# Two transformer blocks on one core: the residual stream kept with its features on the partitions

## What is computed

```python
def _rmsnorm(x, g):
    xf = x.astype(jnp.float32)
    y = xf * lax.rsqrt(jnp.mean(xf * xf, axis=-1, keepdims=True) + RMS_EPS)
    return (y * g.astype(jnp.float32)).astype(x.dtype)

def first_block(...):
    h = x
    h = h + _hybrid_mixer(_rmsnorm(h, norm_mix[l]), w_in[l], ...)
    h = h + _memory_attention(h, mem, norm_mem_q[l], norm_mem_kv[l], w_mem_q[l], w_mem_kv[l], w_mem_o[l])
    h = h + _swiglu(_rmsnorm(h, norm_ffn[l]), w_ffn_in[l], w_ffn_out[l])
    return _rmsnorm(h, norm_final)

def second_block(x, c, w_ada, b_ada, ...):
    mod = einsum(silu(c), w_ada) + b_ada      # 6 x 1024: shifts, scales, gates
    h = _rms(x) * (1.0 + scale_m) + shift_m
    proj = h @ w_in                           # FoX q, k, v, gate, forget; retention q, k, v, gate
    mixed = concat(fox(...), retention(...))
    x = x + gate_m * (mixed @ w_out)
    h = _rms(x) * (1.0 + scale_f) + shift_f
    x = x + gate_f * (square(relu(h @ w_mlp_in)) @ w_mlp_out)
```

## Time and profile before

| | before |
|---|---|
| median of three runs | 883.77 us |
| the three runs | 882.23, 883.77, 889.6 us |
| span of the profiled execution | 881.1 us |
| PE busy | 841.1 us (95%) |
| DVE busy | 591.5 us (67%) |
| ACT busy | 368.0 us (42%) |
| POOL busy | 47.6 us (5%) |
| HBM read | 154.07 MB, 176 GB/s over the span |

### The profile page before, as it was taken

How to read it: one execution, slowest core, us unless ns; L and a number is a source line. 1 busy time by engine, 2 the same in 40 slices (tenths; PEclk the granted TensorE clock), 3 DMA queues, 4 the chain that set the end, 5 groups by cost and what they waited for, 6 DMA issues and landing times.

```text
span 881.1 us, 14098 instructions
## 1 busy us (share of the span) xinstructions
PE 841.1 (95%) x5941; PEld 783.2 (89%) x5941; DVE 591.5 (67%) x873; ACT 368.0 (42%) x469; POOL 47.6 (5%) x59
## 2 busy tenths in 40 slices
PE   6999999999998899999999999999897999999997
PEld 6999898999897889999999799989885999999996
DVE  4967667666685558879786686546666778755553
ACT  5467133653464523333333364445542533343331
POOL 0000000002400000000000200200022000000001
PEclk9999689999998999999999999999899899999999
DMA  8944342242443077676776344342323357645421
GB/s 327 365 170 141 138 144 96 88 152 97 196 187 144 1 278 294 237 295 242 272 298 239 144 144 150 139 145 82 111 96 143 139 197 279 248 152 185 186 96 48
DMA packets 23582, 156.03 MB, mean 177 GB/s; under 512 B 3560, under 2 KB 3808, under 8 KB 5344
## 3 DMA queue, kind: packets, MB, share of 16 engines
q1 hardware_dynamic: 23520, 155.13, 47.9%
HBM read 154.07 MB, written 1.05 MB: 176 GB/s over the span
## 4 chain that ended last, share of the span: by engine, by line
PE 78%; DVE 10%; ACT 5%; issue 3%; POOL 2%; DMA 1%; SPq 0%; DVEq 0%; ACTq 0%; POOLq 0%
PE bank L611 15%; PE bank L612 15%; PE bank L613 15%; PE bank L654 7%; PE bank L655 7%; PE bank L656 7%; PE bank L590 2%; DVE sb_lo L1385 2%; ACT sb_hi L1086 2%; PE bank L840 1%; PE bank L917 1%; PE bank L974 1%; PE bank L950 1%; PE bank L750 1%; POOL sb_fstat L1315 1%
## 5 line engine op out<-in xcount | busy, mean ns | idle before, releaser
L1385 DVE TENSOR_TENSOR sb_lo<-sb_raw,sb_hi 128x2048 fp32r<-128x2048 f32 (+1 forms) x118 | 265.7, 2261 | 118.2 <-ACT sb_hi L1086 118.0
L1086 ACT CAST sb_hi<-sb_raw 128x2048 fp32r<-128x2048 f32 (+1 forms) x118 | 221.4, 1882 | 107.2 <-PE bank L656 80.5
L611 PE MATMUL bank<-sb_u_hi,sb_hi 128*128 128x256 f32 x872 | 251.0, 288 | 0.4 <-DVE sb_u_lo L1453 0.4
L612 PE MATMUL bank<-sb_u_lo,sb_hi 128*128 128x256 f32 x872 | 248.3, 285 | 0.0
L613 PE MATMUL bank<-sb_u_hi,sb_lo 128*128 128x256 f32 x872 | 248.0, 284 | 0.0
L611 PEld LDWEIGHTS bank<-sb_u_hi,sb_hi 128*128 128x128 f32 x872 | 168.0, 193 | 4.8 <-issue 2.9
L612 PEld LDWEIGHTS bank<-sb_u_lo,sb_hi 128*128 128x128 f32 x872 | 168.1, 193 | 1.2
L613 PEld LDWEIGHTS bank<-sb_u_hi,sb_lo 128*128 128x128 f32 x872 | 168.0, 193 | 0.2
L611 PE MATMUL bank<-sb_hi,sb_u_hi 128*128 128x256 f32 (+1 forms) x400 | 116.0, 290 | 1.8 <-DVE sb_u_lo L1448 1.0
L612 PE MATMUL bank<-sb_lo,sb_u_hi 128*128 128x256 f32 (+1 forms) x400 | 113.6, 284 | 0.0
L613 PE MATMUL bank<-sb_hi,sb_u_lo 128*128 128x256 f32 (+1 forms) x400 | 113.6, 284 | 0.0
(11 more groups left out here) (301 smaller groups left out, 946.3 us busy)
## 6 DMA issues: line engine op xcount, KB each, us to landing
sb_raw<-in_stream SPq DMA_DIRECT2D x142, 1024.0 KB, 4.9
sb_h<-in_x SPq DMA_DIRECT2D x2, 512.0 KB, 3.9
sb_mem_rows<-in_mem SPq DMA_DIRECT2D x1, 1024.0 KB, 5.0
out<-sb_h SPq DMA_DIRECT2D x2, 512.0 KB, 2.6
sb_const<-in_constants SPq DMA_DIRECT2D x1, 830.0 KB, 8.9
sb_row_bc<-in_norm_final SPq DMA_DIRECT2D x1, 512.0 KB, 4.6
sb_decays<-in_constants SPq DMA_DIRECT2D x1, 512.0 KB, 8.0
sb_raw<-in_stream SPq DMA_DIRECT2D x1, 320.0 KB, 5.0
```

The costliest lines, as they stand in the source:

```text
L611: nc.tensor.matmul(out, a_hi, b_hi, start=(i == 0), stop=False)
L612: nc.tensor.matmul(out, a_hi, b_lo, start=False, stop=False)
L1086: nc.scalar.copy(hi[:, s % SPLIT, 0:n], x[:, 0:n]).then_inc(sem("hi_ready"), 1)
L1385: tt(lo[:, s % SPLIT, 0:n], x[:, 0:n], f32(hi[:, s % SPLIT, 0:n]), ALU.subtract) \
```

## The change

- `h` has the features on the partitions, [128, 8, 256]; the input `x`, `mem` and all gains and biases (`cols`) are laid out so on the host, and the output is laid back there. The transposes of normalised rows, `xhat` and the row-to-column transpose at the start are gone, and so is `gate_row`: a modulation gate is now one value per partition.
- `accumulate` has the weights as the stationary operand: 48 matmuls of 256 columns for each of the 36 blocks.
- Norms 0 to 3: the products run on `h` times the gain (`u_split`), without the root. Sums of squares go over POOL (adds of 512 columns) and a small matmul (`ssq_cols`); the root is spread over all partitions by a diagonal matrix and a matmul with ones (`rstd_row`) and multiplied to results: `proj` and `mem_v` by ACT with two activations, the gate blocks and `mem_k` by a DVE multiply ahead of the tanh, memory scores by the factor of their scale, `ffn_in` by a DVE multiply of 128x512 (`scale`), whereupon `hidden` (multiply by silu, split) is a step of its own that stands behind the next block's split.
- Norms 5 and 6: squares by ACT, 16 small matmuls, two small DVE instructions, POOL's power, the diagonal, `rstd_row`, a copy, and then for each of eight chunks a DVE multiply, an ACT rounding with the shift and a DVE rest (`u_norm`); the first product goes chunk by chunk (`step`).
- `ada`: 3 in the first projections, 10 in the SwiGLU loop, 6 behind proj2 2, 4, 6, 8, 10 and 12, none in out2.
- Start: `cols` first, then `x` and the first weight block in four pieces each, in turn; warm-ups run on a tile of ones that POOL sets. The small gains of the second block load at ffn_in 7, not 3, `mem` after out 2. The output leaves in four pieces. `IDLE` has fewer places.

```diff
@@ plan
+    def block(*b, evac_now=True, ahead=True):
         s = where[b]
         split(s)
         add("block", s)
         if ahead:
             split(s + 2)
+        if hidden:
+            add("hidden", hidden.pop(0))
+        if evac_now and b[0] not in ("up", "out", "mem_o", "ffn_out", "out2", "mlp_out"):
+            evac(s)
...
+    def normed(n):
+        rstd(n)
+        add("rstd_row", n)
+        for k in range(KD):
+            add("u_norm", n, k)
...
     for i in range(1, 11):
         block("ffn_in", 2 * i)
         more_ada()
         block("ffn_in", 2 * i + 1)
-        if i in (3, 5, 7):
-            more_ada()
-        block("ffn_out", i - 1, evac=False)
+        block("ffn_out", i - 1)
     add("mod", 0)
-    block("ffn_out", 10, evac=False, ahead=False)
+    block("ffn_out", 10, ahead=False)
     table = parts["second"] = []
-    add("residual", 2)
-    norm(5)
-    turn(5)
+    residual(2, 5)
+    normed(5)
     split(where["proj2", 1])
+    add("rstd_row", 4)
     add("final_norm")
...
-             12: [("gate_row", 0), ("mix", 0, 0)]}
+             12: [("mix", 0, 0)]}
     for j in range(13):
         block("proj2", j)
+        if j in (2, 4, 6, 8, 10, 12):
+            more_ada()
@@ IDLE
-IDLE = {("columns",): 10, ("xhat", 0, 0): 4, ("block", 0): 6, ("up", 0, 0): 5, ("out", 0, 0): 18,
-        ("block", MEM_Q): 8, ("mem_o", 0, 0): 5,
-        ("xhat", 3, 0): 6, ("block", FFN_0): 8, ("xhat", 5, 0): 12, ("xhat", 5, 1): 5, ("block", PROJ2_0): 6,
-        ("turn_ret", 2): 8, ("forget_sum",): 9, ("gate_row", 0, 0): 9, 
-        ("xhat", 6, 0): 9, ("block", MLP_0): 8, ("gate_row", 1, 0): 5}
+IDLE = {("block", 0): 16, ("up", 0, 0): 5, ("out", 0): 18, ("mem_o", 0): 5,
+        ("ssq_cols", 5): 4, ("rstd_row", 5): 8, ("block", PROJ2_0): 6,
+        ("turn_ret", 2): 8, ("forget_sum",): 9,
+        ("ssq_cols", 6): 4, ("rstd_row", 6): 8, ("block", MLP_0): 6}
@@ tensor engine, accumulate
-                        for k in range(2):
-                            x1, x2 = x_hi[:, k0 + k, tok], x_lo[:, k0 + k, tok]
-                            nc.tensor.matmul(ps[:, :], x1, w_hi[:, k, n], start=first and k == 0, stop=False)
-                            nc.tensor.matmul(ps[:, :], x1, w_lo[:, k, n], start=False, stop=False)
-                            last = nc.tensor.matmul(ps[:, :], x2, w_hi[:, k, n], start=False,
-                                                    stop=last_one and k == 1)
+                    for m in range(2):
+                        f = slice((2 * c + m) * P, (2 * c + m + 1) * P)
+                        out = ps[:, m * T:m * T + T]
                         for k in range(2):
+                            x1, x2 = x_hi[:, k0 + k, :], x_lo[:, k0 + k, :]
+                            nc.tensor.matmul(out, w_hi[:, k, f], x1, start=(first and k == m == 0), stop=False,
+                                             skip_group_check=True)
+                            nc.tensor.matmul(out, w_hi[:, k, f], x2, start=False, stop=False, skip_group_check=True)
+                            last = nc.tensor.matmul(out, w_lo[:, k, f], x1, start=False, stop=last_one and k == 1,
+                                                    skip_group_check=True)
@@ vector engine
+                if kind == "gate":
+                    ps = wait_filled(dve, ("block", s))
+                    r = rstd_bc[:, ROW_SLOT[0], :].unsqueeze(1).broadcast_to([P, 2, T])
...
+                    free(tt(gates[:, 2 * j:2 * j + 2, :], ps[:, :].rearrange("p (m n) -> p m n", m=2), r, ALU.mult),
+                         ("block", s))
+                    return
...
+            def rstd_row(n):
...
+                dve.wait_ge(sem("rstd_ready"), RSTD_ORDER[n] + 1)
+                r = rstd[:, n, :].unsqueeze(2).broadcast_to([P, NT, P])
+                tt(diag, ident.unsqueeze(1).broadcast_to([P, NT, P]), r, ALU.mult).then_inc(sem(f"diag{n}"), 1)
```

More of the change, by code:

```diff
@@ L129, in split, with evac @@
             split_to[0] += 1
-    def block(*b, evac=True, ahead=True):
+    def evac(s):
+        if blocks[s][0] == "ffn_in":
+            add("scale", s)
+            hidden.append(s)
+        add("evac", s)
+    hidden = []
+    def block(*b, evac_now=True, ahead=True):
         s = where[b]
@@ L238, in plan @@
     for j in range(3):
-        block("up", j, evac=False)
+        block("up", j)
         add("merge", j)
     for j in range(4):
-        block("out", j, evac=False, ahead=j < 3)
-        if j == 0:
-            norm(1)
+        block("out", j, ahead=j < 3)
         if j == 1:
             more_ada()
-        if j == 2:
-            turn(1)
-    add("residual", 0)
-    norm(2)
+            for c in range(4):
+                add("u_split", 1, c)
+            sum_squares(1)
+    residual(0, 2)
     split(where["mem_q",])
-    block("mem_k", ahead=False)
-    turn(2)
+    rstd(1)
+    block("mem_k", ahead=False, evac_now=False)
+    add("rstd_row", 1)
+    evac(where["mem_k",])
+    rstd(2)
     block("mem_q")
@@ L257, in plan @@
     add("turn_o", 3)
-    block("mem_o", evac=False, ahead=False)
-    add("residual", 1)
-    norm(3)
-    turn(3)
+    block("mem_o", ahead=False)
+    residual(1, 3)
     split(where["ffn_in", 1])
@@ L317, in plan @@
     add("mod", 1)
-    add("residual", 3)
-    norm(6)
-    turn(6)
+    residual(3, 6)
+    normed(6)
     split(where["mlp_in", 1])
```

697 lines of the change are left out of this document (396 added, 301 removed).

## The result

The changed kernel takes 939.82 us against 883.62 before (medians), a ratio of 1.0625 (95% interval 1.0582 to 1.0669). Forecast were 903.7 us, 880 to 916: the direction was right, the size was not, by 36 us.

What follows compares the result with a forecast made beforehand. PE, busy 95% of the span, was taken as the bound, with seams left over. Terms sum to 9.7, with proj2 17.4 to 22.4, middle 19.9, on 881.1 us; plus 2.7 for the median gives 903.7 us, range 880 to 916.

Steps and rivals of the forecast that it cites:

- +5.4 for accumulate: 36 accumulate blocks, 48 matmuls of 256 columns instead of 24 of 512: 0.15 us more each, +5.4 us.
- the wait for norm 4's diagonal: Between ffn_out 10 and proj2 0: PE waits some 12 us behind DVE's diagonal; the seam costs +10.0, bounds +4 and +12.
- six modulation blocks in proj2: In the proj2 blocks: six ada of 4.05 us on DVE delay head steps, gate row comes off; +7.7 to +12.7 us.
- gates on DVE, +4.4: Gate blocks: twelve more DVE multiplies of 0.69 us, most in DVE's idle time; +4.4 us, bounds 2.5 and 6.
- memory attention, +0.7: Memory attention: 16 transposes go, but mem_q waits for norm 1's root spread, and half clock adds 0.8; net +0.7 us.
- mem_o to ffn_out 0, −3.5: Seam into the SwiGLU: small gains load moves away, hidden(1) waits for the root; −3.5 us, bounds −7 and 0.
- ffn_out 10, +3.7: Before ffn_out 10: PE waits 3.0 to 3.6 us for hidden(21), with some half clock; +3.7 us.
- t + 9.4: End of DVE's work through scale of 21, counted from t, the end of ffn_in 20.
- the start, −3.4: Start: first product near 6 us, second block near 15, most of 7.8 us gained is lost; −3.4, bounds −7.8 and −2.
- out2 to the end, −5.5: From out2 on: seam by chunks −1.8, gate_row(1) gone −2.8, last adds and store in four pieces −0.9; −5.5 us.
- The fast case: Rival: norm 4's diagonal early, seam +4 at most, six ada within DVE's free 33 us; about 872 us, chance 0.13.
- The slow case: Rival: proj2 chain at +12.7, lower clock behind seams, gates +6, seam +12; about 915 us, chance 0.15.

Runs made afterwards that it cites:

- ada_tail: Changed kernel with the six proj2 modulation blocks each behind the head steps of its block instead of ahead: 925.76 us, ratio 1.0452 to the kernel before.
- gate_defer: Changed kernel with each gate block's evacuation (DVE multiply, ACT tanh) moved to right ahead of the next block: 929.16 us, ratio 1.0537 to the kernel before.
- pool_idle: Changed kernel with POOL's 128x512 work for norms 0 to 3 left out, only the first quarter of squares summed: 924.42 us, ratio 1.0486.
- b_pool: Kernel before with 24 POOL adds of 128x512 from the end of mem_o, which nothing waits for until much later: 894.44 us, ratio 1.0109.
- hid_first: Changed kernel with each hidden step (multiply by silu, split) ahead of the split two blocks on: 928.23 us, ratio 1.0485 to the kernel before.
- ada_stick: Changed kernel with its third modulation block behind the first two stick-breaking heads instead of ahead: 939.09 us, ratio 1.065 to the kernel before.
- b_acc256: Kernel before with each accumulate block as 48 matmuls of 256 columns instead of 24 of 512: 884.66 us, ratio 1.0012.
- b_warm: Kernel before with cols in one load, small gains at ffn_in 7, and 44 instead of 9 warm-ups ahead of norm 6's turn: 878.68 us, ratio 0.9952.
- all_parts: Changed kernel with late norm 4 row, modulation blocks back, POOL's wide sums out, gates without root, hidden ahead of split: 891.92 us, ratio 1.0101.

## Why the prediction was right and wrong

The table sets the terms of the forecast beside what the two traces show for the same stretch of PE. The forecast's two spread terms, +5.4 for accumulate and −2.1 for sums of the modulation, have no row of their own.

| stretch, up to | forecast | measured |
|---|---|---|
| block proj 7 | −3.4 | +2.1 |
| last turn of the heads (the gates) | +4.4 | +11.8 |
| last turn of the memory block | +0.7 | +10.5 |
| ffn_out 0 | −3.5 | +1.6 |
| end of ffn_out 10 | +3.7 | +2.6 |
| start of proj2 0 | +10.0 | +13.7 |
| start of out2 0 | +7.7 to +12.7 | +14.3 |
| the end of the span | −5.5 | −0.4 |

Most of the 36 us are in the first four rows and the last.

**Right: the wait for norm 4's diagonal.** Forecast was that it binds and the seam costs 10; PE waited 10.82 us, and the seam grew by 13.7 (+28.6 to +42.3). One term inside was mis-sized: the small matmuls were put at 0.6 us and take 4.1. PE's weight loads are busy for 4.15 us there, one of 128x128 for each record of two columns, which points to them; no run varied it. Moving the row alone brought 6.3 back, since the chunks behind it need DVE all the same.

**Right in kind, somewhat too small: six modulation blocks in proj2.** The 7.7 to 12.7 of the forecast are net of the gate row's 3.8. Without it they are 11.5 to 16.5, and the two runs gave 16.5 in either layout, the upper end. Net, the stage grew by 14.3 us; the sum had used 10.2. The working knew that forget_sum would come 10 us late (it came 10.0 later after proj2 0 than before, 52.3 against 42.3) and missed what lies behind: another 3.8 us up to L1059, although the gate row is gone there. ada_tail shows that it was the place.

**Wrong: gates on DVE, +4.4, measured 14.1.** The step that failed is "0.7 each" in the chain scores, exp, turn, and that most of the multiplies lie in idle time. DVE had idle time; the multiply stood at the wrong end of it, ahead of a step that PE waits for. gate_defer keeps the work and brings 10.7 us back. Part of the loss may be the clock: three stretches at the lower level between 138 and 167 us that the trace of before did not have.

**Missing: POOL's sums of squares, as a link of the chain and beside DVE.** 15.4 us by pool_idle, and the sum had nothing for it: it is the step that failed in "memory attention, +0.7", which became +10.5 (in pool_idle, 212.26 to 297.18, the stretch is 7.5 us shorter), and behind most of the loss up to ffn_out 0. Without POOL's wide work mem_q starts 7.9 us earlier, of the 21.0 that it came late, and ffn_out 0 17.4 earlier, of 26.0. b_pool shows that POOL's adds beside DVE alone cost 9 us in the kernel before. The price of it could have been read in the trace of before, at POOL's merge of the heads, in timelines of DVE and POOL:

```profile
218.36 2.69 DVE L1385 TENSOR_TENSOR sb_lo<-sb_raw,sb_hi 128x2048 fp32r<-128x2048 f32 x1
```
```profile
218.86 3.33 POOL L1340 TENSOR_TENSOR sb_work<-sb_work,sb_masked 128x512 f32<-128x512 f32 x1
```

The residue takes 2.69 us instead of 2.28, and POOL's add 3.33 instead of 1.28.

**Nearly right at ffn_out 10, +3.7; wrong at mem_o to ffn_out 0, −3.5.** PE waited 2.47 us at ffn_out 10, against 3.0 to 3.6. The parts that the working adds up to t + 9.4 give 9.0, and with that the wait would have been put at 2.6 to 3.2. At ffn_out 0 the hidden step cost 3.90 and norm 3's sums 3.94, so the seam lost 1.6 instead of gaining 3.5 (from +24.4 at the memory block's last turn, 283.86 to 308.29, to +26.0). hid_first brought 11.6.

**Wrong: the start, −3.4.** The first product came at 8.45, where "near 6" was forecast, and block 1 at 20.39 instead of 15.0: ACT's rounding waited until 13.56 for its load, put at 10.6, and POOL's squares held up DVE's splits (18.10 in pool_idle). Then DVE's softplus stood behind the third modulation block: nothing was left by block proj 7 (+2.1), where ada_stick, with the modulation block behind the softplus, starts at 59.70 (−2.2). That the ada takes the gain was seen; that it takes all of it was not.

**Too large: the rate of accumulate, +5.4.** The step that failed compares a product block with an accumulate block and puts the 0.15 us down to the count of matmuls. They differ in more than that. b_acc256 gives 0.08, 2.9 us. In the changed kernel itself a block takes 5.70 us (PE's timeline, an accumulate block and the block behind it), 0.11 more than before, 4.0 in all; what the other 0.03 are stays open.

```profile
899.24 0.28 PE L753 MATMUL bank<-sb_hid_hi,sb_hi 128*128 128x256 f32 x1
...
904.94 0.28 PE L689 MATMUL bank<-sb_u_hi,sb_hi 128*128 128x256 f32 x1
```

**Wrong: out2 to the end, −5.5.** It became −0.4. The first product of the MLP starts at 744.50, 2.3 us closer to out2 than before, but the block goes chunk by chunk and the next one waits 1.94 us for its low part (752.73), so the −1.8 of this seam did not last. The 16 longer accumulate blocks of the MLP take another 1.8. No run took these apart.

**The rivals.** The fast case named the wait at norm 4's row and DVE's 33 free us. The first bound; the second was there and did not help, as the forecast had feared. For the gates and the memory block the forecast counted whether the work fits, and not what stands behind it. The slow case came nearest, but its 915 us, and the range's upper end with it, summed bad ends of known terms, and the largest error was a term that was not there.

**Open.** No run changed the clock alone with success (b_warm did not pay), so its share of the 56 us is not shown; 28 is the bound estimated above. The parts overlap by 12 to 16 us, and I can't say between which. all_parts stays 9 us behind the kernel before; its trace has waits of 4.47 us at norm 1's row and 4.49 at norm 4's, and 36 accumulate blocks that are 0.1 us longer, but no run took those away.

## What to carry to other kernels

On an in-order engine an added instruction costs what stands behind it, not its own length: 0.7 us of work cost 1.2 us each time at one place in the queue and 0.3 to 0.6 at another, though the engine is busy only 66% of the span. So put new work behind the steps that the bound engine waits for, and only then count whether it fits. Before giving GpSimd wide SBUF work, look at what VectorE does beside it: both pay for it, VectorE most where its instructions are short. And set a forecast's terms beside stretches of the trace, net against net, before calling one right.

## What the runs showed of the hardware that was not expected

- DVE instructions of 128x256 with both inputs in SBUF take 1.44 us instead of 0.485 beside POOL adds of 128x512, which take 1.3 to 1.4 there and 3.2 beside a residue of 128x2048; one with an input in a bank keeps 0.42 (b_pool).
- TensorE's clock fell to 0.51 from 103 to 117 us in the kernel before, with PE busy all the time, in a run of matmuls of 16 columns and, behind it, transposes and the first 256-column ones.
- Sixteen float32 matmuls of two columns take 4.1 us, as long as 34 of the 256-column ones at full clock (changed kernel, at 528.42).
- Splitting a 512-column matmul in two of 256 costs 3.3 ns (b_acc256).
- Executions of one kernel differ in their mean clock, and the time goes with it: the profiled one of ada_stick spans 931.4 us at 0.938, three others 937 to 939 at 0.927 to 0.929.
